# Two transformer blocks on one core: ending by tokens, last two ffn output chunks multiplied in quarters; the second sum of squares one feed-forward chunk later

## What is computed

```python
hn = rmsnorm(h, norm2[i])
h = h + jnp.square(jax.nn.relu(hn @ w_up[i])) @ w_down[i]
...
sh1, sc1, g1, sh2, sc2, g2 = jnp.split(mod[:, None, :], 6, axis=-1)
...
x = x + g2 * swiglu(modulate(x, norm2_g[layer], sh2, sc2), w_ffn_in[layer], w_ffn_out[layer])
return rmsnorm_2(x, final_g)
```

## Time and profile before

| what | us |
|---|---|
| median of 3 runs (lowest, highest) | 1266.12 (1266.11, 1269.02) |
| time of the profiled execution | 1265.56 |
| its span | 1263.8 |
| TensorE busy (matmuls) | 1221.8 (97% of the span) |
| VectorE busy | 897.0 (71%) |
| ScalarE busy | 650.3 (51%) |

### The profile page before, as it was taken

How to read it: one execution, slowest core, us unless ns; L and a number is a source line. 1 busy time by engine, 2 the same in 40 slices (tenths; PEclk the granted TensorE clock), 3 DMA queues, 4 the chain that set the end, 5 groups by cost and what they waited for, 6 DMA issues and landing times.

```text
span 1263.8 us, 20995 instructions
## 1 busy us (share of the span) xinstructions
PE 1221.8 (97%) x8494; PEld 1110.8 (88%) x8494; DVE 897.0 (71%) x1284; ACT 650.3 (51%) x994; POOL 96.9 (8%) x84
## 2 busy tenths in 40 slices
PE   8999999999999999999999999979899999999997
PEld 7889899998999889999999989878789998888886
DVE  6887777777888378766657866786476776666665
ACT  6574544446657366454453665542354555344443
POOL 1230000000024020000000000261100000000000
PEclk9999999999999999999999999999999999999999
DMA  9626677666753443655646755332125566655530
GB/s 323 204 88 204 206 244 246 227 222 192 263 175 117 150 135 117 193 174 185 199 150 218 227 174 151 116 100 68 34 97 171 179 230 218 202 181 190 200 133 34
DMA packets 160782, 219.19 MB, mean 173 GB/s; under 512 B 5712, under 2 KB 135598, under 8 KB 160558
## 3 DMA queue, kind: packets, MB, share of 16 engines
q1 hardware_dynamic: 158962, 214.45, 52.3%
q10 hardware_dynamic: 1724, 3.39, 0.7%
HBM read 215.99 MB, written 1.05 MB: 172 GB/s over the span
## 4 chain that ended last, share of the span: by engine, by line
PE 81%; DVE 7%; issue 3%; ACT 3%; DMA 2%; DVEq 1%; ACTq 1%; SPq 1%; POOL 1%; POOLq 1%
PE bank L557 18%; PE bank L559 17%; PE bank L558 17%; PE bank L606 10%; PE bank L608 5%; PE bank L652 2%; DVE w_lo L548 2%; PE bank L918 2%; PE bank L906 1%; PE bank L1481 1%; DMA w_raw<-in_w_in 1%; DMA arena<-arena 1%; DVE arena L1282 1%; PE bank L935 1%; SPq L2949 1%
## 5 line engine op out<-in xcount | busy, mean ns | idle before, releaser
L548 DVE TENSOR_TENSOR w_lo<-w_raw,w_hi 128x1024 fp32r<-128x1024 f32 (+1 forms) x350 | 421.8, 1246 | 56.1 <-ACT w_hi L539 44.7
L539 ACT ACTIVATE w_hi<-w_raw 128x1024 fp32r<-128x1024 f32 (+1 forms) x350 | 350.1, 1041 | 118.3 <-PE bank L559 57.5
L557 PE MATMUL bank<-act_parts,w_hi 128*128 128x256 f32 x1200 | 345.4, 288 | 9.5 <-DVE w_lo L548 7.3
L558 PE MATMUL bank<-act_parts,w_hi 128*128 128x256 f32 x1200 | 340.0, 283 | 0.0
L559 PE MATMUL bank<-act_parts,w_lo 128*128 128x256 f32 x1200 | 340.0, 283 | 0.0
L557 PEld LDWEIGHTS bank<-act_parts,w_hi 128*128 128x128 f32 x1200 | 230.5, 192 | 19.4 <-issue 13.8
L558 PEld LDWEIGHTS bank<-act_parts,w_hi 128*128 128x128 f32 x1200 | 230.8, 192 | 0.7 <-issue 0.2
L559 PEld LDWEIGHTS bank<-act_parts,w_lo 128*128 128x128 f32 x1200 | 230.6, 192 | 0.0
L606 PE MATMUL bank<-act_parts,w_hi 128*128 128x512 f32 x544 | 191.1, 396 | 1.5 <-DVE act_parts L2297 1.4
L608 PE MATMUL bank<-act_parts,w_lo 128*128 128x256 f32 x544 | 151.3, 278 | 0.0
L557 PE MATMUL bank<-w_hi,side_hi 128*128 128x512 f32 (+1 forms) x392 | 149.5, 381 | 0.0
(11 more groups left out here) (345 smaller groups left out, 1625.7 us busy)
## 6 DMA issues: line engine op xcount, KB each, us to landing
w_raw<-in_w_in SPq DMA_DIRECT2D x39, 1024.0 KB, 5.7
w_raw<-in_w_up SPq DMA_DIRECT2D x32, 1024.0 KB, 6.0
w_raw<-in_w_down SPq DMA_DIRECT2D x32, 1024.0 KB, 4.9
w_raw<-in_w_ffn_in SPq DMA_DIRECT2D x22, 1024.0 KB, 5.2
w_raw<-in_w_gate SPq DMA_DIRECT2D x20, 1024.0 KB, 5.2
w_raw<-in_w_mod SPq DMA_DIRECT2D x32, 512.0 KB, 4.0
w_raw<-in_w_ffn_out SPq DMA_DIRECT2D x11, 1024.0 KB, 5.4
w_raw<-in_w_out SPq DMA_DIRECT2D x8, 1024.0 KB, 5.7
```

Source lines behind the costliest of these rows:

```text
L539: nc.scalar.activation(whi[:, slot, 0:n], raw[:, st.slot(name), n * half:n * (half + 1)], ACT.Copy).then_inc(hi_ready, 1)
L548: nc.vector.tensor_tensor(wlo[:, slot, 0:n], raw[:, st.slot(name), n * half:n * (half + 1)], whi[:, slot, 0:n].bitcast(F32), ALU.subtract) ...
L557: nc.tensor.matmul(o, ahi, bhi, start=start, stop=False, skip_group_check=True)
L558: nc.tensor.matmul(o, ahi, blo, start=False, stop=False, skip_group_check=True)
```

## The change

- SSQ2_AT goes from 3 to 4: `sum_squares(2)` moves, in both layers, from the end of step up2 to step up3, there ahead of the relu's square, and TensorE's matmul for it from after up3 to after up4. The terms start one up step later. Layer 0 makes up for it with a term in out step 10 and one in up2 in place of up1; layer 1 with one in down11.
- The order of the last feed-forward chunks is now a9 b9 a10 b10 out8 out9 out10. out8 is multiplied as before. out9 and out10 are multiplied together in four quarters, one bank after the other (`project_quarters`), each followed by a semaphore. The activations of chunk 10 lie in another buffer (`ple_hi`, `ple_lo`).
- The ending stays in token rows. Ahead of the feed-forward TensorE turns `h` to token rows (`h_by_tokens`, 16 transposes: 12 after the norm's sum, 4 after b0), and ScalarE copies them. For each quarter VectorE multiplies the bank with the gate as a row, adds the row of `h`, and multiplies with the final gain as a row. ScalarE squares with an accumulated sum, and takes Ln and Exp of 128 x 1 values. Each engine scales one half of the channels, and four stores of 256 KB go out.
- For this the gate is made as a row: modulation 10 and 11 are summed and spread to all partitions by one matmul with a constant column (`quad`) and 512 columns in place of the four transposes. Two loads of 512 KB spread the rows of the bias and of the final gain over the partitions; they stand in SP's queue behind chunk 24 of the second block and wait for `o_done`.

```diff
-SSQ2_AT = 3
+SSQ2_AT = 4
...
+NFF = FF2 // 256
+OUTS_AFTER = [[]] + [[j - 1] for j in range(1, NFF - 2)] + [[], [NFF - 3, NFF - 2, NFF - 1]]
...
-for i, at in enumerate([11, 12, up_at(1)] + [up_at(j) for j in range(3, UPS)]):
+for i, at in enumerate([10, 11, 12, up_at(2)] + [up_at(j) for j in range(4, UPS)]):
...
-for i, at in enumerate([up_at(j) for j in range(3, UPS)] + [down_at(j) for j in (12, 13, 14)]):
+for i, at in enumerate([up_at(j) for j in range(4, UPS)] + [down_at(j) for j in (11, 12, 13, 14)]):
...
+        def project_quarters(pe, names, parts, ready, quarter_done):
+            for t in range(TT):
+                tok = slice(P * t, P * (t + 1))
+                for n in range(2):
+                    w = slice(512 * n, 512 * (n + 1))
+                    for i, name in enumerate(names):
+                        if t == n == 0:
+                            ready(i)
+                        hi, lo = parts[i]
+                        for half in range(2):
+                            slot = st.piece(name, half)
+                            if t == n == 0:
+                                pe.wait_ge(lo_ready, st.pieces(name, half))
+                            mm = three(pe, ps[2 * n + t][:, :], hi[half][:, tok], lo[half][:, tok],
+                                       whi[:, slot, w], wlo[:, slot, w], start=False,
+                                       stop=i == len(names) - 1 and half == 1)
+                    mm.then_inc(quarter_done, 1)
...
+                if j >= 10:
+                    full(nc.tensor.matmul(ps[b][:, :], col("quad").broadcast_to([P, P]), rows_of(j), start=True, stop=True), b)
+                    return
...
# ScalarE
+                if j == NFF - 1:
+                    nxt(l + 1)
                 act.wait_ge(S("ff_p"), j + 1)
...
+            nxt(l + 1)
+            for t in range(TT):
+                for n in range(2):
+                    act.wait_ge(S("y_steps"), 4 * t + 2 * n + 1)
+                    of = slice(512 * n, 512 * (n + 1))
+                    nc.scalar.activation(pre_x.rearrange("p k t -> p (k t)")[:, of], y_rows[:, t, of],
+                                         ACT.Square, accum_out=(tok_part, tok_sum)[n][:, t:t + 1])
...
+                nc.scalar.activation(tok_sum[:, t:t + 1], tok_sum[:, t:t + 1], ACT.Ln, scale=1.0 / D,
+                                     bias=tok_part[:, t:t + 1])
+                act.drain()
+                nc.scalar.activation(tok_rstd2[:, t:t + 1], tok_sum[:, t:t + 1], ACT.Exp, scale=-0.5)
+                act.drain().then_inc(S("post_rstd"), 1)
+                act.wait_ge(S("y_steps"), 4 * t + 2)
+                nc.scalar.activation(ff_out[:, t, 0:512], ff_out[:, t, 0:512], ACT.Copy,
+                                     scale=tok_rstd2[:, t:t + 1]).then_inc(S("y_act"), 1)
...
# VectorE, mod_sum
+                if j >= 10:
+                    of = slice(512 * (j - 10), 512 * (j - 9))
+                    dve.wait_ge(S("row_landed"), 32)
+                    free(v.tensor_tensor(gate_row[:, of], ps[b][:, :], b_mod_row[:, of], ALU.add), b)
+                    return
...
# VectorE, the ending
+            for t in range(TT):
+                for n in range(2):
+                    of = slice(512 * n, 512 * (n + 1))
+                    dve.wait_ge(S("ffo_quarter"), 2 * t + n + 1)
+                    v.tensor_tensor(ff_out[:, t, of], ps[2 * n + t][:, :], gate_row[:, of], ALU.mult)
+                    dve.drain()
+                    v.tensor_tensor(y_rows[:, t, of], y_rows[:, t, of], ff_out[:, t, of], ALU.add)
+                    dve.drain().then_inc(S("y_steps"), 1)
+                    v.tensor_tensor(ff_out[:, t, of], y_rows[:, t, of], final_row[:, of], ALU.mult)
+                    dve.drain().then_inc(S("y_steps"), 1)
+                dve.wait_ge(S("post_rstd"), 4 + t)
+                v.tensor_scalar(ff_out[:, t, 512:D], ff_out[:, t, 512:D], tok_rstd2[:, t:t + 1], None, ALU.mult)
+                dve.drain().then_inc(S("y_dve"), 1)
...
# SyncE
+                if name == ("post", ROWS_AT):
+                    sp.wait_ge(S("o_done"), 1)
+                    for to, first in ((b_mod_row, V["b_mod_2"] + 40), (final_row, V["final_g_2"])):
+                        row = a["vec_rows"][first:first + KT, :]
+                        sp.dma_start(to, bass.AP(row.tensor, row.offset, [[0, P], [1, D]])).then_inc(S("row_landed"), 16)
...
+            for t in range(TT):
+                for n, said in enumerate(("y_act", "y_dve")):
+                    of = slice(512 * n, 512 * (n + 1))
+                    sp.wait_ge(S(said), t + 1)
+                    sp.dma_start(y[:, t, of], ff_out[:, t, of]).then_inc(S("stored"), 16)
```

More of the change, by code:

```diff
@@ L481, in two_blocks @@
             ffn += [k_all(a["w_ffn_in_2"][0], 256 * j), k_all(a["w_ffn_in_2"][0], FF2 + 256 * j)]
[L482 to L484 removed]
+            for i in OUTS_AFTER[j]:
+                ffn += [k_rows(a["w_ffn_out_2"][0], 256 * i)]
         post_src += ffn
@@ L1803, in _, with h_by_tokens @@
             sum_tiles(C("norm2"), pre_x, "sq_tiles", 4, 2)
+            def h_by_tokens(t, half, bank):
+                b = banks.claim(pe, f"h_tok{t}{half}", bank)
+                for i in range(4):
+                    mm = tr(ps[b][:, P * i:P * (i + 1)], h[:, 4 * half + i, P * t:P * (t + 1)])
+                full(mm, b)
+            h_by_tokens(0, 0, 0)
+            h_by_tokens(0, 1, 1)
+            h_by_tokens(1, 0, 2)
             mod_chunk(22, lambda: 3)
@@ L1823, in _ @@
                     l += 1
-                if j:
-                    ffn_out(j - 1, l)
+                if j == 0:
+                    h_by_tokens(1, 1, 3)
+                for i in OUTS_AFTER[j][:1]:
+                    ffn_out(i, l)
                     l += 1
[L1827 to L1834, removed]
-                for t in range(TT):
-                    c = 2 * half + t
-                    pe.wait_ge(S("y_cols"), 4 * (half + 1))
-                    b = C(f"y_out{c}")
-                    for k in range(4):
-                        mm = tr(ps[b][:, P * k:P * (k + 1)], h[:, 4 * half + k, P * t:P * (t + 1)])
-                    full(mm, b)
+            project_quarters(pe, [("post", l), ("post", l + 1)], [ff_parts(nff - 2), ff_parts(nff - 1)],
+                             lambda i: pe.wait_ge(S("ff_act"), nff - 1 + i), S("ffo_quarter"))
         @block.scalar
@@ L2246, in _ @@
                 nxt(l)
+                if j < 2:
+                    for t, half in (((0, 0), (0, 1), (1, 0)), ((1, 1),))[j]:
+                        b = W(f"h_tok{t}{half}")
+                        free(nc.scalar.activation(y_rows[:, t, 512 * half:512 * (half + 1)], ps[b][:, :], ACT.Copy), b)
+                    act.drain().then_inc(S("h_tok"), 1)
                 act.wait_ge(S("ff_sum"), j + 1)
@@ L2256, in _ @@
                     nxt(l)
                     l += 1
-            nxt(l)
-            for n in range(2):
-                if n == 0:
-                    act.wait_ge(S("ffo_half"), 1)
-                else:
-                    done(l)
-                free(nc.scalar.activation(ffo_rows[2 * n], ps[2 * n][:, :], ACT.Copy), 2 * n)
-                act.drain().then_inc(S("ffo_act"), 1)
-            for c in range(4):
-                square_pair(c, 4 + c + 1)
-            rms(W("final2"), T, 1.0 / D, rstd[:, :]).then_inc(S("post_rstd"), 1)
@@ L2841, in _ @@
                 l += 1
-                if j:
+                if j < NFF - 1 and OUTS_AFTER[j]:
                     nxt(l)
                     l += 1
-            for n in range(2):
-                if n == 0:
-                    dve.wait_ge(S("ffo_half"), 1)
-                else:
-                    done(l)
-                free(v.tensor_copy(ffo_rows[2 * n + 1], ps[2 * n + 1][:, :]), 2 * n + 1)
-                dve.drain().then_inc(S("ffo_dve"), 1)
-            for c in range(4):
-                residual(W(f"h5{c}"), c, 40)
@@ L2854, in _ @@
-            dve.wait_ge(S("post_rstd"), 4)
-            for k in range(KT):
-                v.scalar_tensor_tensor(h[:, k, :], h[:, k, :], vcol("final_g_2", k), rstd[:, :], ALU.mult,
-                                       ALU.mult).then_inc(S("y_cols"), 1)
-            for c in range(4):
-                if c % 2 == 1:
-                    b = W(f"y_out{c}")
-                    free(v.tensor_copy(y_rows[:, c % 2, 512 * (c // 2):512 * (c // 2 + 1)], ps[b][:, :]), b)
-                    dve.drain().then_inc(S(f"y_rows{c // 2}"), 1)
+            nxt(l + 1)
```

52 lines of the change are left out of this document (29 added, 23 removed).

## The result

| | median, us (lowest, highest; runs) | profiled execution | its span |
|---|---|---|---|
| before | 1266.11 (1265.82, 1269.02; 4) | 1265.56 | 1263.8 |
| changed | 1255.77 (1254.50, 1256.21; 4) | 1255.37 | 1253.5 |

The ratio is 0.9912, 95% interval 0.9894 to 0.9929: 10.3 us less. The forecast was 8.0 less, 1258.1, with a range from 1256.3, so the gain was underrated by 2.3 us and the result lies just outside.

The account below looks back on a forecast made before the run. TensorE's work and gaps were taken to bound the kernel until its last weight matmul, then a serial ending of 16.9 us. Terms -1.4 + 1.5 - 8.1 = -8.0 gave 1258.1 us against the median, range 1256.3 to 1260.3.

Parts of the forecast that it names:

- layer 0: Moving the sum of squares closes TensorE's gaps of 0.40 and 1.01 us: -1.4 us, bounds -1.4 and 0.
- layer 1: The same move delays a relu's square by 2.4 us at most: taken as 0, +1.0 as bound against.
- the work added to TensorE: 16 transposes, 12 of them covered, and the gate's two row matmuls: +1.5 us, bounds +1.2 and +1.9.
- the ending: Quarters and token rows shorten the serial row after the last weight matmuls: -8.1 us, bounds -9.5 and -6.0.
- Row loads: Two 512 KB loads in SP's queue take 5.2 us, leaving 11.7 of lead: cost 0.
- Rival 4: Row loads are slow and delay the gate chunks and TensorE by 17.5 us: 1275.6 us; chance 0.02.
- The new wait in the first quarter: TensorE waits for the split of out10's second half, which uses out8's buffers: 0.6 us, bounds 0 and 1.5.
- The stores: At the end, 256 KB stores land no faster than 512 KB ones, 2.7 us; the span ends 3.1 after 1252.6.
- Rival 1: The last stores' landing grows with their size, saving 0.4 to 1.25 us, say 0.6: 1257.5 us; chance 0.15.
- Rival 2: Layer 0's gaps close, but TensorE's gain is waited for again later: 1259.5 us; chance 0.10.
- Rival 3: The ending is less short: out10's split later (1.5 for 0.6), stores following by 1.6 for 0.4: 1260.2; chance 0.08.
- Rival 5: First quarters come no sooner than the whole, as VectorE takes them up only after out10's split; no own chance.

Follow-up runs that it names:

- experiment 1: The kernel before with only the moved sum of squares and terms in both layers, old ending: 1263.91 us, ratio 0.9972.
- experiment 3: The changed kernel with layer 1's sum of squares and terms as before: 1257.6 us, ratio 0.9925.
- experiment 6: The changed kernel with ScalarE scaling both channel halves of the first token half: 1256.12 us, ratio 0.9910.
- Experiment 7: The changed kernel with one store of 512 KB a token half in place of two of 256: 1257.17 us, ratio 0.9917.

## Why the prediction was right, and where it was wrong

The mechanisms were those forecast. What failed is the size of four terms of the sum: layer 0 (-1.87 for -1.4), layer 1 (-0.41 for 0), the work added to TensorE (+1.27 for +1.5) and, the largest, the ending (-8.95 for -8.1). All four errors go the same way, 2.0 us together, and that took the result out of the range.

- **Layer 0, -1.4.** A-B measured 1.85 to 1.92 less whichever two profiles are compared. The step that failed is "bounds -1.4 and 0": I took the printed idle, 1.01 and 0.40, as the gap, and as the most that could be gained. The bracket counts from the modelled end of the matmul before, 0.39 after its start, while the next one would have started 0.23 after it. In the trace of before the last matmul ahead of 143.97 started at 142.57: 1.40 less 0.23 is 1.17, and the first matmul behind the wait is followed at 0.19 in place of 0.12, so 1.24. The other gap gives 131.50 - 130.71 - 0.23 + 0.07 = 0.63. Together 1.87.
- **Layer 1, 0.** It measured -0.41 (D-E, experiments 1 and 3). I looked for idle in brackets and took the row's move for a risk alone, with +1.0 as the bound. The chain of waits shows the same sum of squares ahead of the same split, and I had read that view only for the ending. A bound below nothing was due here as well.
- **Work added to TensorE, +1.5.** By its own rows it is +1.27: 0.42 and 0.41 for the row matmuls, forecast at 0.55 each, and 0.44 for the four transposes, as forecast. The 12 transposes cost nothing, their cover held. The stretches are too noisy to price it alone: E-F, where the first row matmul lies, is 0.3 to 0.7 more in the table; F-G, with the second and the four transposes, is +1.02 between the first pair of profiles and 0.4 in the mean of the table's later ones, under a scatter of 0.9. Inside the bounds of 1.2 and 1.9, but 0.2 too high.
- **Row loads, 0.** Right; they took 7.4 in place of 5.2, inside the 11.7 of lead. Rival 4 fell: six of them cost nothing either.
- **The new wait in the first quarter, 0.6.** The bracket says 0.34 at 1237.01. The distance from the matmul before it, 0.74, is 0.51 more than the pace, and the next one follows 0.1 later than usual, 0.6 in all; quarter 2 was taken up at G + 6.11 for a forecast of 6.09. Right.
- **The ending, -8.1.** G-H went from 27.79 to 18.87, -8.92. The forecast had 19.69. Of the 0.82 between, 0.22 lay before quarter 3: ScalarE's row from square to Exp took 1.36 where I had added up 1.6 with gaps of 0.1, and the scaling 0.49 of my 0.5 to 0.69. Gate and add took 1.53 for 1.64 (the product with its drain 0.77, where 0.82 was taken from another step), and ScalarE's last row 1.45 for 1.6. The largest part, 0.4, is the last store. VectorE was behind at quarter 4 by 0.5 (experiment 6), for a forecast of 0.8.
- **The stores.** "2.7 for 512 KB and also 2.7 for a first load of 131 KB" made me take the size for nothing. That first load takes 2.3 to 2.8 over the fourteen profiles, and it is no store: a weak basis. Experiment 7 shows 2.6 against 2.1 for stores. Rival 1 was right in its mechanism and right to expect 0.4 or more on top of the forecast.
- **Rival 2 and 3** fell, by experiment 1 and by G-H. Rival 5 fell: VectorE idled 1.12 before quarter 1.

By these terms the change is worth -1.87 - 0.41 + 1.27 - 8.95 = -9.96 (8.95 is the difference between the means of G-H in the table). The three comparisons of medians gave -10.3, -10.3 and -9.9. The range failed because it was built of whole rivals: its low end lies 1.8 below the forecast, the far ends of the bounds were left out, and the bounds of the two layers had no room for a larger gain at all.

## What to carry to other kernels

A gap's price is the distance from start to start less the pace, not the bracketed idle: here each wait of TensorE was worth 0.2 to 0.3 more than its bracket said, and one showed no bracket at all; the chain of waits shows it. When two kernels are compared by one profile each, measure between the same marks of the program, and believe the stretches that repeat. In an ending where engines alternate, take the work off the engine that is last to be free (0.5 us here) before removing another engine's wait: done by an order that brings the first quarter later, that made it worse (0.45 us); done by one that keeps the first quarter where it was, it gave another 0.6.

## What the runs showed of the hardware

In layer 1 TensorE sits idle for some 2.1 us at mark C. In six of the fourteen profiled executions its granted clock was low right after it (0.62 to 0.70 in the window below), in eight not (1.00), whichever the kernel: before once and not once, the change once and not twice. Busy time of each engine in one stretch (PE, PEld, DVE, ACT, POOL, granted clock, DMA share, GB/s), changed kernel, second execution:

```profile
459.50:464.00 4.50, 4.40 (x25) 4.40 (x26) 2.97 (x8) 2.49 (x7) 0.00 (x0) 0.62 0.75 233
```

and third:

```profile
459.50:464.00 4.50, 4.50 (x39) 4.33 (x38) 2.76 (x7) 2.56 (x8) 0.00 (x0) 1.00 0.73 227
```

TensorE in order of time, second execution:

```profile
459.60 0.66 PE L871 MATMUL bank<-consts_sb,arena 128*128 128x128 f32 x4 [2.12 <-DVE arena L1226]
...
461.63 0.41 PE L561 MATMUL bank<-act_parts,w_hi 128*128 128x256 f32 x1
461.84 0.41 PE L562 MATMUL bank<-act_parts,w_lo 128*128 128x256 f32 x1
```

and third:

```profile
459.30 0.66 PE L871 MATMUL bank<-consts_sb,arena 128*128 128x128 f32 x4 [2.07 <-DVE arena L1226]
...
460.99 0.28 PE L561 MATMUL bank<-act_parts,w_hi 128*128 128x256 f32 x1
461.11 0.28 PE L562 MATMUL bank<-act_parts,w_lo 128*128 128x256 f32 x1
```

The matmuls follow at 0.21 in place of 0.12, the lower of the clock's two levels, and C-D takes 31.5 in place of 30.15: 1.4 us that an execution pays or doesn't, after the same idle (2.08 with the drop in the kernel before, 2.07 without). What decides it stays open.

F-G, where TensorE never waits, took 171.2 to 172.2 on the first chip and 173.2 to 174.0 on the three others, at a granted clock shown as 1.00 in all of them. What makes the difference isn't shown. With start-up (A from 80.9 to 82.5) and C-D this is why a single profile can't tell a microsecond, and a stretch of it that repeats can tell a tenth.
